# Second down-projection of a two-layer trunk in fp32r on one core: one product for all tokens in tiles 0 to 6, the last tile by halves of the tokens

## The reference, cut to what matters

```python
def rms_norm(x, gain):
    x32 = x.astype(jnp.float32)
    y = x32 * lax.rsqrt(jnp.mean(x32 * x32, axis=-1, keepdims=True) + RMS_EPS)
    return (y * gain.astype(jnp.float32)).astype(x.dtype)

def conv_ffn(h, w_up, conv_w, w_down):
    up = h @ w_up
    ...
    gate, val = jnp.split(up, 2, axis=-1)
    return (jax.nn.silu(gate) * val) @ w_down
...
        h = h + conv_ffn(rms_norm(h, ffn_norm[layer]), ffn_w_up[layer], ffn_conv[layer], ffn_w_down[layer])
    return rms_norm(h, final_norm)[:, N_META:]
```

## Time and profile before

| what | value |
|---|---|
| time, median of 3 runs | 1174.3 us (1174.24 to 1175.01) |
| the profiled execution's own time | 1173.89 us |
| its span, first to last instruction | 1172.1 us |
| granted TensorE clock, mean over the span | 0.972 of 2.4 GHz |
| PE busy, share of the span | 95% |
| last product of the last tile ends | 1159.30 us |
| first of the four stores is issued | 1165.15 us |

### The profile page before, as it was taken

The page is one execution under the profiler, slowest core; times in us unless marked ns, Lnnn a source line. Parts: engine busy times, 40 slices in busy tenths (PEclk is TensorE's granted clock), DMA queues, the critical chain, the costliest instruction groups (busy, mean ns, idle before and its releaser), DMA issues.

```text
span 1172.1 us, 28346 instructions
## 1 busy us (share of the span) xinstructions
PE 1114.4 (95%) x10546; PEld 1094.1 (93%) x10546; DVE 496.8 (42%) x853; ACT 485.5 (41%) x883; POOL 639.8 (55%) x540
## 2 busy tenths in 40 slices
PE   4588899999999999999999999999999999999996
PEld 3577899999999999999999999999999999999996
DVE  7986312354444444301116777344444444421101
ACT  4843333354444444322324545444444444432222
POOL 4994355455555555665444445656555555565551
PEclk7589999999999999999999999999999999999998
DMA  7048633233333333332223433323333333333321
GB/s 153 23 121 173 170 91 89 73 99 89 89 89 89 89 89 98 104 94 87 86 72 92 96 80 83 99 81 100 87 93 89 92 93 92 103 99 99 89 60 72
DMA packets 221974, 110.51 MB, mean 94 GB/s; under 512 B 33271, under 2 KB 219527, under 8 KB 221591
## 3 DMA queue, kind: packets, MB, share of 16 engines
q1 hardware_dynamic: 214823, 105.41, 32.6%
q10 hardware_dynamic: 7090, 4.26, 1.4%
HBM read 103.31 MB, written 6.32 MB: 94 GB/s over the span
## 4 chain that ended last, share of the span: by engine, by line
PE 88%; POOL 6%; ACT 1%; DMA 1%; DVE 1%; issue 1%; SPq 0%; ACTq 0%; DVEq 0%; POOLq 0%
PE slot L1227 82%; PE slot L1368 1%; PE slot L1419 1%; DMA xc<-in_x 1%; POOL cpow L1934 1%; POOL ptmp L1933 1%; POOL cpow L1932 1%; POOL cpow L1929 1%; POOL cpow L1931 1%; POOL ptmp L1930 1%; PE slot L1420 1%; PE slot L1398 1%; PE slot L1148 1%; PE slot L1142 1%; DMA gelu_scratch<-x_raw 0%
## 5 line engine op out<-in xcount | busy, mean ns | idle before, releaser
L1965 POOL TENSOR_TENSOR w_lo<-raw,w_hi 128x512 fp32r<-128x512 f32 (+2 forms) x312 | 430.7, 1383 | 422.2 <-ACT w_hi L635 411.7
L635 ACT ACTIVATE w_hi<-raw 128x512 fp32r<-128x512 f32 (+2 forms) x308 | 203.0, 663 | 401.9 <-PE slot L1227 391.7
L1227 PE MATMUL slot<-xa_hi,w_hi 128*128 128x264 f32 (+1 forms) x1472 | 298.6, 284 | 0.9 <-DVE xa_lo L1720 0.9
L1227 PE MATMUL slot<-xa_hi,w_lo 128*128 128x264 f32 (+1 forms) x1472 | 298.4, 284 | 0.0
L1227 PE MATMUL slot<-xa_lo,w_hi 128*128 128x264 f32 (+1 forms) x1472 | 298.1, 284 | 0.0
L1227 PEld LDWEIGHTS slot<-xa_hi,w_hi 128*128 128x128 f32 x1472 | 229.0, 189 | 1.3 <-issue 1.1
L1227 PEld LDWEIGHTS slot<-xa_lo,w_hi 128*128 128x128 f32 x1472 | 228.3, 189 | 0.0
L1227 PEld LDWEIGHTS slot<-xa_hi,w_lo 128*128 128x128 f32 x1472 | 227.8, 189 | 0.0
L1227 PE MATMUL slot<-act_hi,w_hi 128*128 128x264 f32 (+1 forms) x704 | 141.7, 282 | 0.0
L1227 PE MATMUL slot<-act_lo,w_hi 128*128 128x264 f32 (+1 forms) x704 | 141.5, 282 | 0.0
L1227 PE MATMUL slot<-act_hi,w_lo 128*128 128x264 f32 (+1 forms) x704 | 141.2, 282 | 0.0
(11 more groups left out here) (285 smaller groups left out, 1486.9 us busy)
## 6 DMA issues: line engine op xcount, KB each, us to landing
raw<-in_ffn_w_up SPq DMA_DIRECT2D x176, 256.0 KB, 2.9
raw<-in_ffn_w_down SPq DMA_DIRECT2D x32, 384.0 KB, 3.4
raw<-in_ffn_w_down SPq DMA_DIRECT2D x32, 320.0 KB, 3.0
raw<-in_s_w_glu SPq DMA_DIRECT2D x32, 256.0 KB, 2.8
toep<-kern_scratch SPq DMA_DIRECT2D x64, 64.0 KB, 2.9
raw<-in_w_q SPq DMA_DIRECT2D x16, 256.0 KB, 3.1
raw<-in_w_o SPq DMA_DIRECT2D x16, 256.0 KB, 2.9
gelu_scratch<-x_raw ACTq DMA_DIRECT2D x8, 264.0 KB, 2.7
```

What stands on the lines that cost most here:

```text
L635: run(buffer_of(w_hi_all, buf, nk), buffer_of(raw_all, buf, nk), ACT.Copy).then_inc(hi_done, 1)
L1227: ins = mm(slot[dst][:, half, 0:b - a], w, xx[:, k, a:b], start=k == 0 and n == 0, stop=k == nk - 1 and n == 2)
L1965: tt(buffer_of(w_lo_all, buf, nk), buffer_of(raw_all, buf, nk), f32(buffer_of(w_hi_all, buf, nk)), ALU.subtract).then_inc(lo_done, 1)
```

## The change

In tiles 0 to 6 of dn1 `REAL_TOKENS` becomes a single stretch of 512 tokens, so a tile is 66 products of 512 columns into one PSUM bank. DVE reads it from there (`real_of`).

The last tile is taken out of the loop. It makes all 66 products of the first 256 tokens (`last_tile(0, ...)`), then all 66 of the others (`last_tile(1, ...)`), and each half has its own residual add, square, gain, transposes, statistics, root, reciprocal, scaling and stores. The statistics add `acc` of tiles 0 to 6 and the square of tile 7 by two accumulating products for each block, so POOL does not add the last square any more. The transposes of tile 6 move from behind the last tile's products to behind its first six blocks. SP's stores now go in the order 1, 0, 3, 2.

```diff
-REAL_TOKENS = ((META, MID), (MID, L))
+REAL_TOKENS = ((META, L),)
+
+LAST_HALVES = ((META, MID), (MID, L))
...
-        real_of = lambda n: slot[n][:, :, 0:SEQ // 2]
+        real_of = lambda n: slot[n][:, 0, 0:SEQ]
+        half_of = lambda half: slot[1][:, half, 0:SEQ // 2]
...
-            for n in range(4):
+            for n in (1, 0, 3, 2):
                 sp.wait_ge((scaled_act, scaled_dve)[n % 2], n // 2 + 1)
...
+            def last_square(half):
+
+                a, b = LAST_HALVES[half]
+                act.wait_ge(h_done["dn1"], KD + half)
+                act.wait_ge(acc_done["dn1"], KD - 2)
+                run(sq[:, 1, a:b], h[:, KD - 1, a:b], ACT.Square).then_inc(sq_done["dn1"], 1)
+
+            def last_copy(half):
+
+                act.wait_ge(ot_full, KD + half)
+                run(otok[:, 2 * half:2 * half + 2, (KD - 1) * P:KD * P],
+                    slot[2 + half][:, 0, 0:2 * P].rearrange("p (n c) -> p n c", n=2), ACT.Copy).then_inc(ot_copied, 1)
...
+                for half in range(2):
+                    last_square(half)
+                    final_rms(half)
+                    last_copy(half)
+                    final_scale(half)
...
+            def last_tile(half, k0, k1):
+
+                a, b = LAST_HALVES[half]
+                if half == 0 and k0 == 0:
+                    pe.wait_ge(h_done["dn1"], KD - 2)
+                for k in range(k0, k1):
+                    if half == 0 and k in W_AT:
+                        c = S_DN1 + 4 * (KD - 1) + W_AT.index(k) + 1
+                        pe.wait_ge(hi_done, c)
+                        pe.wait_ge(lo_done, c)
+                    hi, lo = w_hi_all[:, k * P:(k + 1) * P], w_lo_all[:, k * P:(k + 1) * P]
+                    for n, (w, xx) in enumerate(((hi, act_hi), (hi, act_lo), (lo, act_hi))):
+                        ins = mm(half_of(half), w, xx[:, k, a:b], start=k == 0 and n == 0, stop=k == KF - 1 and n == 2)
+                if k1 == KF:
+                    ins.then_inc(last_full, 1)
...
+            def final_statistics(half):
+
+
+                a = LAST_HALVES[half][0]
+                pe.wait_ge(acc_done["dn1"], KD - 1)
+                pe.wait_ge(sq_done["dn1"], KD + half)
+                for n in range(2):
+                    sums = slot[2 + half][:, 1, n:n + 1]
+                    mm(sums, acc[:, a + n * P:a + (n + 1) * P], ones[:, 0:1], start=True, stop=False)
+                    ins = mm(sums, sq[:, 1, a + n * P:a + (n + 1) * P], ones[:, 0:1], start=False, stop=True)
+                ins.then_inc(fin_full, 1)
+
             down("dn1", S_DN1, "up1", REAL_TOKENS, hook)
-            out_tile(KD - 1, 1)
-
-            pe.wait_ge(acc_done["dn1"], KD)
-            for n in range(4):
-                ins = mm(slot[3][:, 1, n:n + 1], acc[:, META + n * P:META + (n + 1) * P], ones[:, 0:1],
-                         start=True, stop=True)
-            ins.then_inc(fin_full, 1)
+            last_tile(0, 0, W_AT[1])
+            out_tile(KD - 2, 0)
+            last_tile(0, W_AT[1], KF)
+            last_tile(1, 0, GRP)
+            final_statistics(0)
+            last_transposes(0)
+            last_tile(1, GRP, KF)
+            final_statistics(1)
+            last_transposes(1)
...
+            for half, (a, b) in enumerate(LAST_HALVES):
+                dve.wait_ge(last_full, half + 1)
+                tt(h[:, KD - 1, a:b], half_of(half), h[:, KD - 1, a:b], ALU.add).then_inc(h_done["dn1"], 1)
...
+                dve.wait_ge(fin_rms, half + 1)
+                two = rinv[:, 2 * half:2 * half + 2]
+                nc.vector.reciprocal(two, two).then_inc(fin_rinv, 1)
+                dve.wait_ge(fin_rinv, half + 1)
+                dve.wait_ge(ot_copied, KD + half)
+                n = 2 * half + 1
                 ts(otok[:, n, :], otok[:, n, :], rinv[:, n:n + 1], None, ALU.mult).then_inc(scaled_dve, 1)
```

More of the change, by code:

```diff
@@ L402, in trunk @@
             sem(n) for n in ("pt_full", "pt_copied", "pv_done", "ao_hi_done", "ao_lo_done"))
-        hg_done, ot_full, ot_copied, fin_full, fin_rms, fin_rinv, scaled_act, scaled_dve, written = (
-            sem(n) for n in ("hg_done", "ot_full", "ot_copied", "fin_full", "fin_rms", "fin_rinv", "scaled_act",
+        last_full, hg_done, ot_full, ot_copied, fin_full, fin_rms, fin_rinv, scaled_act, scaled_dve, written = (
+            sem(n) for n in ("last_full", "hg_done", "ot_full", "ot_copied", "fin_full", "fin_rms", "fin_rinv", "scaled_act",
                              "scaled_dve", "written"))
@@ L923, in up, with final_rms, final_scale @@
                 act_copy(KF - 1)
+            def last_square(half):
[7 more added lines that the diff above has]
+                    slot[2 + half][:, 0, 0:2 * P].rearrange("p (n c) -> p n c", n=2), ACT.Copy).then_inc(ot_copied, 1)
+            def final_rms(half):
+                act.wait_ge(fin_full, half + 1)
+                run(rinv[:, 2 * half:2 * half + 2], slot[2 + half][:, 1, 0:2], ACT.Sqrt, scale=1.0 / D,
+                    bias=eps[:, :]).then_inc(fin_rms, 1)
+            def final_scale(half):
+                n = 2 * half
+                act.wait_ge(fin_rinv, half + 1)
+                act.wait_ge(ot_copied, KD + half)
+                run(otok[:, n, :], otok[:, n, :], ACT.Copy, scale=rinv[:, n:n + 1]).then_inc(scaled_act, 1)
             def down(p, base, g, nxt):
@@ L945, in down @@
                 tile(KD - 1, 1, nxt)
-                residual(p, KD - 1, 1, g)
-                if p == "dn1":
-                    out_copy(KD - 1, 1)
+                if p == "dn0":
+                    residual(p, KD - 1, 1, g)
+                    return
+                for half in range(2):
[3 more added lines that the diff above has]
+                    final_scale(half)
             def out_copy(m, par):
@@ L1024, in _ @@
             down("dn1", S_DN1, None, None)
[L1026 to L1030, removed]
         @block.tensor
@@ L1323, in down @@
                 tile(1, 1)
-                with pe.Fori(1, KD // 2) as i:
+                with pe.Fori(1, KD // 2 - (p == "dn1")) as i:
                     for e in range(2):
                         tile(pe.snap(i * 2 + e), e)
+                if p == "dn1":
+                    tile(KD - 2, 0)
             def attention():
@@ new lines, in last_transposes @@
+            def last_transposes(half):
+                a = LAST_HALVES[half][0]
+                pe.wait_ge(hg_done, KD + half)
+                pe.wait_ge(ot_copied, KD - 2 + half)
+                for n in range(2):
+                    ins = tr(slot[2 + half][:, 0, n * P:(n + 1) * P], sig[:, 1, a + n * P:a + (n + 1) * P], ident[:, :])
+                ins.then_inc(ot_full, 1)
+            def final_statistics(half):
+                a = LAST_HALVES[half][0]
+                pe.wait_ge(acc_done["dn1"], KD - 1)
+                pe.wait_ge(sq_done["dn1"], KD + half)
+                for n in range(2):
+                    sums = slot[2 + half][:, 1, n:n + 1]
+                    mm(sums, acc[:, a + n * P:a + (n + 1) * P], ones[:, 0:1], start=True, stop=False)
+                    ins = mm(sums, sq[:, 1, a + n * P:a + (n + 1) * P], ones[:, 0:1], start=False, stop=True)
+                ins.then_inc(fin_full, 1)
@@ L1693, in update @@
                 first, product = {"dn0": (0, acc_of), "o": (LIVE, live_of), "dn1": (META, real_of)}[p]
-                hm = halves(tile_of(h, m, first))
+                hm = tile_of(h, m, first) if p == "dn1" else halves(tile_of(h, m, first))
                 tt(hm, product(e), hm, ALU.add).then_inc(h_done[p], 1)
@@ L1874, in out_update @@
                 ts(sig[:, e, :], tile_of(h, m), column(gain(G_FIN), m), None, ALU.mult).then_inc(hg_done, 1)
[L1876 to L1881, removed]
+            out_update(0, 0)
+            out_update(1, 1)
+            with dve.Fori(1, KD // 2 - 1) as i:
+                for e in range(2):
+                    out_update(dve.snap(i * 2 + e), e)
+            out_update(KD - 2, 0)
+            for half, (a, b) in enumerate(LAST_HALVES):
+                dve.wait_ge(last_full, half + 1)
+                tt(h[:, KD - 1, a:b], half_of(half), h[:, KD - 1, a:b], ALU.add).then_inc(h_done["dn1"], 1)
+                dve.wait_ge(h_done["dn1"], KD + half)
+                if half == 0:
+                    dve.wait_ge(ot_full, KD - 2)
+                ts(sig[:, 1, a:b], h[:, KD - 1, a:b], column(gain(G_FIN), KD - 1), None, ALU.mult).then_inc(hg_done, 1)
+                dve.wait_ge(fin_rms, half + 1)
[4 more added lines that the diff above has]
+                n = 2 * half + 1
                 ts(otok[:, n, :], otok[:, n, :], rinv[:, n:n + 1], None, ALU.mult).then_inc(scaled_dve, 1)
@@ L2052, in down @@
                 loop_2(KD, tile)
-                add_square(p, KD - 1, 1)
+                if p == "dn0":
+                    add_square(p, KD - 1, 1)
             def attention():
```

## The result

The changed kernel takes 1169.95 us (median of 6, 1168.3 to 1170.56), the kernel before 1174.44 us beside it (median of 6). The ratio is 0.9956, with a 95% interval of 0.9946 to 0.9966. That is 4.5 us faster, clear of the 0.2%, where 7.3 us were forecast and the range ended at 1169.0.

A forecast was written before the change was run, and what follows sets the result against it. PE, busy for 95% of the span, was taken as the bound, with a chain of short steps behind it. Terms -5.1 + 2.3 - 4.5 = -7.3 us gave a median of 1167.0 us, range 1161.5 to 1169.0.

The forecast's parts named there:

- the merge of tiles 0 to 6: dn1 tiles 0 to 6: 12 ns fixed per product, 225.3 ns at 512 columns, 14.87 us a tile, 5.1 us saved.
- The second rival: dn1 merge: cost belongs to the columns, 512 take twice 256, nothing saved by merging; 1172.1 us, chance 0.08.
- The page's 2.5 ns: Trainium skill's warm step, N/2.4 + 2.5 ns: 215.8 ns at 512 columns, 9.5 us saved over seven tiles.
- The last tile: PE ahead of its last product: moved transposes, statistics and two stalls add 2.3 us, bounds 1.6 and 3.3.
- The 0.4 us for `sig`: Last tile: PE stalls 0.4 us at tile 6's moved transposes, waiting for `sig`, taken as 1.67 us long.
- The other stall: Last tile: PE waits 0.3 us for the first half's square before its statistics, beyond nine covering products.
- The end: Behind the last product: 8.26 us instead of 12.80, so 4.5 us shorter, bounds 3 and 5.2.
- Weights that keep pace: dn1: ACT's weight splits stay ahead of PE with tiles of 14.9 us, no cost.
- The cheap product (2.5 ns): Rival, dn1 merge: fixed cost mostly goes away, 215.8 ns at 512 columns, 9.5 us saved; 1162.6 us, chance 0.10.
- The merge without any gain: The second rival's claim for dn1: 512 columns take twice 256, so merging saves nothing; 1172.1 us, chance 0.08.
- The stalls that grow: Rival, last tile or behind it: a wait is 2 to 4 us longer; 1169 to 1171 us, chance 0.08.
- the 241 at which the change would have lost: Rival, slower: 512-column products below a column a cycle; a loss from 241 ns on, about 1266 us at 439 ns, chance 0.03.

The follow-up runs named there:

- merge_only: Kernel before with all eight dn1 tiles, the last too, as 66 products of 512 columns and the old end: 1173.23 us, ratio 0.9985.
- The two uneven cuts: Kernel before with dn1's 512 tokens cut 384 + 128 or 448 + 64 instead of 256 + 256: 1202.71 and 1216.32 us.
- the bf16 probes: merge_only with dn1's products reading fixed bf16 buffers, at 512 columns and at 256 + 256: 1176.3 and 1173.88 us, one execution each.
- before_again: Kernel before, unaltered, run and profiled a second time: 1173.91 us, ratio 0.9993.
- split_only: Changed kernel with tiles 0 to 6 again as 132 products of 256 columns, last tile still by halves: 1172.06 us, ratio 0.9979.
- early_stats: Changed kernel with the first half's statistics and transposes right behind its last product, ahead of the nine covering products: 1171.76 us, one execution.

## Why the prediction was wrong

**The step that failed is the merge of tiles 0 to 6.** It was put as "I take 12 ns", a fixed time "for each product whatever its width", so 225.3 ns at 512 columns and 5.1 us saved. merge_only and the profile after have 230.9 ns and 0.35 us a tile, 2.4 us for seven. The three widths from which the 12 ns came lie within 3% of each other. There they can't tell a cost of the product from one of the columns, and "lie nearest to a cost for each product" was a choice without ground. The second rival drew a line through 256 and 264 columns (240 ns at 512) and was set aside because "that lever is too short". The lever was short, but a cost that grows with the columns was there: 230.9 ns lies between that line and the forecast. The two uneven cuts bear it out, with pairs that fit a line through 256 and 512 to 1 ns. The page's 2.5 ns was compared with the rows and found too low, which was right for this type; the bf16 probes meet it to 0.1 ns.

**A second part is the range's upper end.** It held only the terms of dn1 and the end. The 1.3 us between 5.4 and 4.1 us in the profiles come from the start-up, whose scatter the three times given before (0.8 us apart) did not show. The later runs of the same kernel before lie 4.4 us apart. With the median of 4.5 us and the interval of the ratio (4.0 to 6.3 us) the 5.4 us of the stages agree, so no further loss has to be explained.

**The last tile: right in kind, 1.7 for 2.3 us.** Statistics, two transposes and the four moved ones cost 1.5 us where 1.6 were worked out, and the stalls were 0.16 us and not 0.7.

The 0.4 us for `sig` fell away because the row was taken over with its slow 1.67 us. Tile 6 now stands behind DVE's loop, and the register step of that line in the loop (0.08 us) is in the trace six times before and four after. `sig` starts 0.04 us after the add (0.26 idle before), ahead of POOL's `w_lo`, and takes 0.50 us. The prediction held that the neighbour stays, and a shift of 0.35 us undid it. That it is the order and not the merge shows in merge_only, whose merged tile 6 is still in the loop:

```profile
1144.01 1.67 DVE L1874 TENSOR_SCALAR sig<-h,gains 128x528 f32 x1 [0.26 <-DVE h L1695]
```

```profile
1143.81 1.58 POOL L1965 TENSOR_TENSOR w_lo<-raw,w_hi 128x640 fp32r<-128x640 f32 x1 [1.89 <-ACT w_hi L635]
```

The kernel before had both kinds already. Its tiles 0 and 1 stand outside the loop, and their `sig` takes 0.50 us beside POOL's 1.77:

```profile
1048.30 0.50 DVE L1874 TENSOR_SCALAR sig<-h,gains 128x528 f32<-128x528 f32 x1
```

```profile
1048.46 1.77 POOL L1965 TENSOR_TENSOR w_lo<-raw,w_hi 128x640 fp32r<-128x640 f32 x1 [1.99 <-ACT w_hi L635]
```

Over tiles 0 to 6 of the profiles of before, before_again, merge_only, after and split_only, all 12 that start 0.15 us ahead of `w_lo` take 0.50 us, and all 23 that start 0.17 to 0.29 us behind it take 1.57 to 1.69.

The other stall was over by half, since the square came sooner. PE could go on at 1.06 us behind the half's last product and not at 1.20. The nine products covered it up to 0.91, as worked out (0.89). DVE started 0.04 us behind the product and not 0.15, and ACT 0.03 behind the add and not 0.12: the DVE row that the first was read from stands in the loop, with its register step ahead of it. Why ACT follows sooner is not shown. split_only has the same 17.27 us.

**The end: right, 4.8 for 4.5 us.** The steps came in the order worked out and a little sooner: the square ends at 0.9 us (forecast 1.14) and the two blocks are scaled from 2.85 (3.10), the table load in the first half alone, the stores bound by two times 1.29 us of data behind the first issue (3.7 us, forecast 3.9). The first half's stores were done before.

**Weights that keep pace: right.** No row of the changed kernel has PE waiting for `w_hi` or `w_lo` in dn1.

**The rivals.** The cheap product (2.5 ns) did not come. The merge without any gain did not either, but the cost that grows with the columns, on which it stood, is there. The stalls that grow did not show in this kernel; early_stats shows that they would have cost more than their length. The product of 512 columns is 15.1 ns above bf16, and 10 ns below the 241 at which the change would have lost.

## What to carry to other kernels

A cost per instruction that is read from instructions of nearly the same size is not a cost per instruction: when a merge doubles the size, keep a straight line through the known widths as one end of the range, and measure the new width in a probe if you can. A duration taken from a row holds only with its neighbours, so ask what else moves by a few tenths of a us. And put the scatter of a kernel's latency-bound start into the range of any forecast of a few us, from more than three runs.

## What the runs showed that was not expected

- fp32r products step by 118.1 ns at 256 columns and 230.9 at 512, bf16 by 109.2 and 215.8. Merging two fp32r products of 256 columns into one of 512 saves 5.3 ns, in bf16 2.6.
- Uneven cuts are dear. 384 + 128 columns take 286.5 ns for a pair and 448 + 64 take 314.5, against 236.2 for 256 + 256: each narrow product costs some 110 ns, with 128 columns as with 64.
- The same DVE instruction takes 0.50 us when it starts 0.15 us ahead of POOL's `w_lo`, and 1.57 to 1.69 when it starts 0.17 to 0.29 behind it.
- In one execution the granted clock fell from 1.00 to 0.54 in the middle of a dense stretch, behind 1.06 us of idle time and one-column products. With a stall of 0.16 us ahead of the same products it stayed at 1.00.
- The start of dn1 in one program, unaltered, differed by 1.5 us between two executions, and the time from there to the end by 0.1.
